# Experts in a mixture layer: row units of 128, 144 and 152 rows in place of 128 and 152

## The chip, the core and the metric

The kernel runs on one core of a Trainium2 chip. The metric is the device time of one launch in microseconds. Three runs of the kernel before gave 4332.75, 4333.61 and 4339.43 us; their median, 4333.61 us, is its time. The profiled execution took 4334.02 us, and its span, from the first to the last recorded instruction, is 4332.2 us. Engines are called as in the profile: PE (matmul) with PEld (its weight loads), DVE (vector), ACT (scalar), POOL (GpSimd) and SP (which issues most DMAs).

## What is computed

512 tokens of width 1024 in fp32 run through two blocks: retention and gated attention, a dense feed-forward, a second gated mixer, a mixture of experts, then a second block with two kinds of attention and a lookup of expert rows (called `peer` in the names). The change is in the mixture of experts:

```python
def moe_swiglu(h, w_router, w_gate, w_up, w_down):
    logits = (xt @ w_router).astype(jnp.float32)          # 512 x 8
    top_logits, top_idx = lax.top_k(logits, TOP_K)         # 2 of 8
    gates = jax.nn.softmax(top_logits, axis=-1)
    order = jnp.argsort(top_idx.reshape(-1))
    group_sizes = jnp.bincount(flat_e, length=N_EXPERTS)
    xs = xt[order // TOP_K]                                # 1024 rows, by expert
    hid = silu(ragged_dot(xs, w_gate, group_sizes)) * ragged_dot(xs, w_up, group_sizes)
    ys = lax.ragged_dot(hid, w_down, group_sizes)          # weights 1024x3584 and 3584x1024 per expert
```

The 1024 rows (512 tokens, two experts each) spread over eight experts as the router decides. On the inputs of the reference its router gives the experts 0 to 7 these numbers of rows: 137, 118, 116, 149, 142, 117, 118, 127.

## The kernel before

Routing, up to the counts, is done at run time: `Router.route` (L1667 to 1757) on DVE takes the two best of eight logits per token, counts the rows of each expert (`count`), and decides with which units an expert is computed. An expert with at most 128 rows takes one unit of 128 rows (kind A), one with more takes units of 152 (kind B). `need` holds the units per expert and kind, `upto` their running sum, `owner` the expert of each unit, `begin` the first row of an expert in the list of rows. The list `token_of_row` in DRAM has a region for each kind: A from row 0, B from row `FIRST_ROW[1]` = 1024. Once the casts to `R.units` and `R.expert` are done (L1722, L1724), every engine reads the number of units of each kind into a register (`expert_values`, lower bound 1) and loops over them. The rest of the routing makes `router_here`, a 0/1 matrix by which PE gathers the rows of the first unit (L1649), and the row numbers, by which POOL scatters the tokens to the list (L1661).

A unit goes through the 3584 hidden columns of its expert in 14 groups of 256. For each group SP loads 1 MB of gate, up and down weights (L1869, L1870, L1876) into one of two rooms, as soon as PE frees it. PE multiplies, for each half j of 128 columns, 8 gate and 8 up matmuls (L1891; the weights are stationary, the unit's rows the moving columns), ACT takes silu (L1984), DVE multiplies (L2014), and PE adds the down product. Kind A has the hidden rows as stationary and 512 weight columns moving (L1908); kind B has the weights stationary and its rows moving (L1921), so that its output is transposed. At the end of a B unit DVE copies the sums to `yT` (L2042), PE turns them back (L1974), and ACT stores them to `y_rows`; meanwhile POOL has fetched the next unit's rows by an index (L1800, L1804), PE turns them (`turn`, L1816) and DVE places them (`place`, L1827). Groups 1 to 12 of a unit run in an inner loop of six passes with two groups each, the units of a kind in an outer loop. First all A units run, then all B units.

`y_rows` (3072 rows, `ROWS_MAX`) is blanked by one DMA from SP (L582), issued in the retention stage at 220 us and waited for at the end of the gated stage behind it (`Clears.end`, L587). Kinds have their own rooms and signals (`ExpertRows`).

Of the kernel before, what the change touches and what calls it, by code (L numbers as in the profile page):

```python
# [33 lines left out]
UNIT_ROWS = (P, 152)  # L34
GROUP = 256
UNITS_MAX = (N_EXP, (2 * T + (N_EXP - 1) * (UNIT_ROWS[1] - 1)) // UNIT_ROWS[1])
FIRST_ROW = (0, UNITS_MAX[0] * UNIT_ROWS[0])
ROWS_MAX = (FIRST_ROW[1] + UNITS_MAX[1] * UNIT_ROWS[1] + P - 1) // P * P
# [1547 lines left out]
class Router:  # L1586
# [19 lines left out]
    def rooms(self, st):  # L1606
# [14 lines left out]
        self.need = S.sb("router_need", [P, 2, N_EXP], F32, st)  # L1621
        self.large = S.sb("router_large", [P, N_EXP], F32, st)
        self.begin = S.sb("router_begin", [P, 2, N_EXP], F32, st)
        self.more = S.sb("router_more", [P, N_EXP], F32, st)
        self.upto = S.sb("router_upto", [P, 2, N_EXP], F32, st)
# [4 lines left out]
        self.past = S.sb("router_past", [P, 2, 16, N_EXP], F32, st)  # L1630
        self.owner = S.sb("router_owner", [P, 2, 16], F32, st)
# [34 lines left out]
    def route(self, dve):  # L1666
        S, R, nc, ps, own = self.S, self.R, self.S.nc, self.S.ps, self.own  # L1667
        lg, top, top_i, top_f, hot, both, e2 = self.lg, self.top, self.top_i, self.top_f, self.hot, self.both, self.e2
        need, large, begin, more, upto, first, pos = self.need, self.large, self.begin, self.more, self.upto, self.first, self.pos
# [42 lines left out]
        dve.wait_ge(own.sem, o.value())  # L1712
        nc.vector.tensor_tensor(begin[:, :, :], upto[:, :, :], need[:, :, :], ALU.subtract).then_inc(own.sem, o.up())
        for c in range(2):
            nc.vector.tensor_tensor(self.past[:, c, :, :], S.const("iota16").unsqueeze(2).broadcast_to([P, 16, 8]),
                                    upto[:, c, :].unsqueeze(1).broadcast_to([P, 16, 8]), ALU.is_ge).then_inc(own.sem, o.up())
# [8 lines left out]
        for c in range(2):  # L1725
            nc.vector.tensor_scalar(begin[:, c, :], begin[:, c, :], float(UNIT_ROWS[c]), float(FIRST_ROW[c]), ALU.mult,
                                    ALU.add).then_inc(own.sem, o.up())
# [3 lines left out]
        nc.vector.tensor_tensor(begin[:, 0, :], begin[:, 0, :], need[:, 0, :], ALU.mult).then_inc(own.sem, o.up())  # L1731
        nc.vector.tensor_tensor(begin[:, 1, :], begin[:, 1, :], large[:, :], ALU.mult).then_inc(own.sem, o.up())
        dve.wait_ge(own.sem, o.value())
        nc.vector.tensor_tensor(first[:, :], begin[:, 0, :], begin[:, 1, :], ALU.add).then_inc(own.sem, o.up())
        dve.wait_ge(own.sem, o.value())
# [29 lines left out]

class ExpertRows:


    def __init__(self, S, R, size, st):
        self.S, self.R = S, R  # L1770
        self.unfetched = 1 if size == 0 else 0
        self.rows, self.row0 = UNIT_ROWS[size], FIRST_ROW[size]
        self.subs = [(r0, min(P, self.rows - r0)) for r0 in range(0, self.rows, P)]
        self.bank0 = (2, 4)[size]
        n = len(self.subs)
        self.xg = S.sb(f"rows{size}_x", [P, n, D], F32, st)
        self.xu = S.sb(f"rows{size}_xt", [P, KD, self.rows], F32, st)
# [11 lines left out]

    def units(self, eng):  # L1790
        size = 0 if self.row0 == 0 else 1
        return expert_values(eng, self.R.units[0:1, size:size + 1], 1, UNITS_MAX[size])

    def fetch(self, pool, u):
        S, nc, R, n_subs = self.S, self.S.nc, self.R, len(self.subs)

        pool.wait_ge(self.turned.sem, self.turned.at(2 * n_subs * u))
        settle(pool, S.sig("passed_pool"))
        for s, (r0, n) in enumerate(self.subs):
            pool.dma_start(self.index[0:n, s:s + 1], R.token_of_row[bass.ds(u * self.rows + self.row0 + r0, n), :]).then_inc(self.indexed.sem, 16)  # L1800
        pool.wait_ge(self.indexed.sem, self.indexed.at(16 * n_subs * (u + (1 - self.unfetched))))
        settle(pool, S.sig("passed_pool"))
        for s, (r0, n) in enumerate(self.subs):
# [4 lines left out]
    def turn(self, pe, u):  # L1808
        S, nc = self.S, self.S.nc
        pe.wait_ge(self.gathered.sem, self.gathered.at(16 * len(self.subs) * (u + (1 - self.unfetched))))  # L1810
        settle(pe, S.sig("passed_pe"))
        for s, (r0, n) in enumerate(self.subs):
# [7 lines left out]
    def place(self, dve, u):  # L1820
        S, nc, n_subs = self.S, self.S.nc, len(self.subs)
        for s, (r0, n) in enumerate(self.subs):
            for half in range(2):
                dve.wait_ge(self.turned.sem, self.turned.at(2 * n_subs * u + 2 * s + half + 1))
# [5 lines left out]
    def store(self, act, u):  # L1830
        for s, (r0, n) in enumerate(self.subs):
            act.dma_start(self.R.y[bass.ds(u * self.rows + self.row0 + r0, n), :], self.yrow[0:n, s, :]).then_inc(self.stored.sem, 16)


def experts_stage(S, R, router, xn):
# [5 lines left out]
    with ExitStack() as st:  # L1841
# [3 lines left out]
        gs = S.sb("experts_gs", [P, 2, UNIT_ROWS[1]], F32, st)  # L1845
        hid = S.sb("experts_hid", [P, 2, UNIT_ROWS[1]], F32, st)
        yT = S.sb("experts_yt", [P, KD, UNIT_ROWS[1]], F32, st)
        zero = S.sb("experts_zero", [P, BANK], BF16, st)
        A, B = ExpertRows(S, R, 0, st), ExpertRows(S, R, 1, st)
        router.rooms(st)  # L1850
        routed = router.routed

        with nc.Block("experts") as block:
            @block.sync
            def _(sp):
                def unit(E, size, u, others=None, n_others=0):
                    e = expert_values(sp, R.expert[0:1, size, bass.ds(u, 1)], 0, N_EXP - 1)
                    g, up, dn = (a[w][0][bass.ds(e, 1)].rearrange("o a b -> (o a) b")
                                 for w in ("moe_w_gate", "moe_w_up", "moe_w_down"))
                    with sp.Fori(0, per) as i:  # L1860
                        for b in range(2):
# [3 lines left out]
                            sp.wait_ge(E.freed[b].sem, E.freed[b].at(u * per + i))  # L1865
# [8 lines left out]
                            sp.wait_ge(E.down_freed[b].sem, E.down_freed[b].at(u * per + i))  # L1874
# [4 lines left out]
                n_a, n_b = A.units(sp), B.units(sp)  # L1879
                with sp.Fori(0, n_a) as u:  # L1880
                    unit(A, 0, u)
                with sp.Fori(0, n_b) as u:
                    unit(B, 1, u, A, n_a)

            @block.tensor
            def _(pe):
                def gate_up(E, b, n, j):
                    pe.wait_ge(E.hidden[j].sem, E.hidden[j].at(n))
                    for w, bank in ((wg, 4 + j), (wu, 6 + j)):
                        for k in range(KD):  # L1890
                            ins = nc.tensor.matmul(ps[bank][:, 0:E.rows], w[:, b, k, j * P:(j + 1) * P], E.xu[:, k, :],  # L1891
# [22 lines left out]
                def down_b(b, u, i, n):  # L1914
                    for j in range(2):
                        pe.wait_ge(B.hidden[j].sem, B.hidden[j].at(n + 1))
                        if j == 0:
                            pe.wait_ge(B.down_loaded[b].sem, B.down_loaded[b].at((u * per + i + 1) * 16))
                        for d in range(KD):
                            at = (d % 2) * B.rows  # L1920
                            ins = nc.tensor.matmul(ps[d // 2][:, at:at + B.rows], wd[:, b, j, d * P:(d + 1) * P], hid[:, j, :],  # L1921
                                                   start=False, stop=False, skip_group_check=True)
                            if j == 0 and d == 0:
                                ins.then_inc(B.freed[b].sem, 1)
                    ins.then_inc(B.down_freed[b].sem, 1)
# [3 lines left out]
                n_a, n_b = A.units(pe), B.units(pe)  # L1929
# [20 lines left out]
                with pe.Fori(0, n_b) as u:  # L1950
                    pe.wait_ge(B.x_ready.sem, B.x_ready.at(4 * u + 4))
                    settle(pe, S.sig("passed_pe"))
                    n0 = u * n_groups
                    first_half(B, 0, u, 0, n0)
                    pe.wait_ge(B.emitted.sem, B.emitted.at(4 * u))
                    for bank in range(4):
                        nc.tensor.matmul(ps[bank][:, :], zero[:, 0:P], zero[:, :], start=True, stop=False, skip_group_check=True)
                    down_b(0, u, 0, n0)
                    with pe.Fori(0, per - 1) as i:
                        first_half(B, 1, u, i, n0 + i * 2 + 1)  # L1960
                        down_b(1, u, i, n0 + i * 2 + 1)
                        first_half(B, 0, u, i + 1, n0 + i * 2 + 2)
                        down_b(0, u, i + 1, n0 + i * 2 + 2)
                    first_half(B, 1, u, per - 1, n0 + last)
# [1828 lines left out]
```

## Time and profile before

| | us |
|---|---|
| median of three runs | 4333.61 |
| profiled execution | 4334.02 |
| its span | 4332.2 |
| expert units, 128 rows (5) | 1307.6 to 2067.4 |
| expert units, 152 rows (3) | 2067.4 to 2603.5 |

The page of the profile gives the busy time of each engine over the span, and a strip of 40 slices of 108 us, each digit a busy share in tenths. Views by window give the same for any stretch, with the granted clock of PE (1.00 is 2.4 GHz) and the share and rate of the DMA engines. The timeline lists instructions in order of time, with start and length, merged when they repeat (xN), and in brackets how long the engine had been idle before and what released it. An fp32 matmul leaves two records. A length of one matmul includes its way through the array, so the distance from one start to the next is what it costs in a stream.

### The profile page before, as it was taken

The numbers are of one execution on the slowest core, as the hardware profiler recorded it, in microseconds if no ns is written. First come the engines' busy times: TensorE is split into PE (matmuls) and PEld (weight loads), VectorE is DVE, ScalarE is ACT, GpSimd is POOL, SyncE is SP. The second block draws the span as 40 slices with busy tenths as digits, with TensorE's granted clock in tenths as the row PEclk, the third lists the DMA queues.
The fourth block names the chain that finished last, engine by engine and source line by source line (L and its number), as shares of the span: only waits on it lengthen the run. The fifth ranks groups of instructions, "written<-read, shape, count | busy, mean of one in ns | idle before, by whom it ended". The sixth has DMA issues, their size and how long they took to land. (4 is left out here: it accounts for less than half of the span.)

```text
span 4332.2 us, 45502 instructions
## 1 busy us (share of the span) xinstructions
PE 3776.8 (87%) x17099; PEld 2506.9 (58%) x17106; DVE 1706.8 (39%) x3683; ACT 626.6 (14%) x1566; POOL 1095.9 (25%) x1162
## 2 busy tenths in 40 slices
PE   7989999999989999999999996998866777666666
PEld 3465777744747888888999993465422222222222
DVE  2051231013730000000000004748887776877655
ACT  1121000013520000000000003143211111111011
POOL 0010000001400000000000000003667777777775
PEclk9989999999989999999999998989888888888888
DMA  3143675230019888898777764036899999999998
GB/s 114 48 166 120 229 257 189 98 136 0 20 68 275 306 294 303 306 311 298 254 258 250 257 215 140 25 103 240 337 392 386 418 416 414 419 416 416 419 415 355
DMA packets 549127, 1092.57 MB, mean 252 GB/s; under 512 B 37577, under 2 KB 336982, under 8 KB 548870
## 3 DMA queue, kind: packets, MB, share of 16 engines
q1 hardware_dynamic: 395802, 539.66, 36.8%
q0 software_dynamic: 150768, 546.25, 31.3%
q10 hardware_dynamic: 2428, 5.03, 0.3%
q8 instruction: 69, 1.13, 0.1%
q14 instruction: 60, 0.49, 0.0%
HBM read 1069.55 MB, written 21.30 MB: 252 GB/s over the span
## 5 line engine op out<-in xcount | busy, mean ns | idle before, releaser
L3224 PE MATMUL banks<-peer_ring,consts 128*128 128x512 f32 x1512 | 846.9, 721 | 372.8 <-DMA peer_ring<-in_peer_v_dram,peer_expert 372.8
L3224 PEld LDWEIGHTS banks<-peer_ring,consts 128*128 128x128 f32 x1512 | 339.2, 232 | 875.1 <-DMA peer_ring<-in_peer_v_dram,peer_expert 465.2
L3425 DVE SCALAR_TENSOR_TENSOR peer_ring<-peer_ring,banks 128x1024 f32<-128x1024 f32 x512 | 594.1, 1217 | 252.4 <-DMA peer_ring<-in_peer_u_dram,peer_expert 251.5
L3128 POOL DMA_INDIRECT peer_ring<-in_peer_u_dram,peer_expert x512 | 482.4, 942 | 546.3 <-POOLq L2745 347.1
L3128 POOL DMA_INDIRECT peer_ring<-in_peer_v_dram,peer_expert x512 | 490.6, 958 | 170.1 <-issue 142.5
L2014 DVE TENSOR_TENSOR experts_hid<-experts_gs,banks 128x128 f32<-128x128 f32 (+1 forms) x224 | 66.7, 298 | 1175.9 <-ACT experts_gs L1984 1175.9
L1891 PEld LDWEIGHTS banks<-rows_xt,experts_wg 128*128 128x128 f32 x3584 | 446.9, 192 | 45.2 <-issue 45.1
L1891 PE MATMUL banks<-rows_xt,experts_wg 128*128 128x128 f32 (+1 forms) x3584 | 462.3, 282 | 11.3 <-DMA experts_wu<-in_moe_w_up_dram 9.3
L1891 PE MATMUL banks<-rows_xt,experts_wu 128*128 128x128 f32 (+1 forms) x3584 | 461.3, 282 | 0.0
L1891 PEld LDWEIGHTS banks<-rows_xt,experts_wu 128*128 128x128 f32 x3584 | 441.2, 192 | 0.0
L405 PE MATMUL banks<-xT,proj_w 128*128 128x512 f32 (+1 forms) x720 | 319.6, 601 | 8.2 <-PEq L3576 4.8
L1800 POOL DMA_DIRECT2D rows_index<-token_of_row x13 | 7.4, 575 | 1061.2 <-PE banks L1816 1043.0
L1908 PE MATMUL banks<-experts_wd,experts_hid 128*128 128x512 f32 x560 | 251.9, 592 | 0.0
L405 PEld LDWEIGHTS banks<-xT,proj_w 128*128 128x128 f32 (+1 forms) x720 | 135.5, 190 | 185.2 <-issue 183.9
L1023 POOL TENSOR_TENSOR hgrn_both<-k,hgrn_diff 128x256 f32<-128x256 f32 x56 | 44.3, 814 | 772.7 <-ACT hgrn_diff L934 761.6
L1984 ACT ACTIVATE experts_gs<-banks 128x128 f32<-128x128 f32 (+1 forms) x224 | 63.9, 285 | 1183.1 <-PE banks L1891 1183.0
L3456 DVE SCALAR_TENSOR_TENSOR banks<-peer_ring,peer_wgt,banks 128x1024 f32<-128x1024 f32 x130 | 167.5, 1288 | 79.3 <-DMA peer_ring<-in_peer_v_dram,peer_expert 78.7
L1921 PE MATMUL banks<-experts_hid,experts_wd 128*128 128x152 f32 x1344 | 180.5, 293 | 0.0
L1921 PEld LDWEIGHTS banks<-experts_hid,experts_wd 128*128 128x128 f32 x1344 | 176.3, 190 | 0.4
L408 PE MATMUL banks<-proj_w,xT 128*128 128x512 f32 (+1 forms) x448 | 174.1, 548 | 0.0
L1357 PE MATMUL banks<-xT,ffn_wg 128*128 128x256 f32 x704 | 161.3, 383 | 1.2 <-ACT ada_c L1395 1.2
L1431 DVE TENSOR_TENSOR ffn_hid<-ffn_gs,banks 128x256 f32<-128x256 f32 x44 | 18.5, 422 | 360.9 <-ACT ffn_gs L1401 360.9
(506 smaller groups left out, 3754.7 us busy)
## 6 DMA issues: line engine op xcount, KB each, us to landing
experts_wg<-in_moe_w_gate_dram SPq DMA_DIRECT2D x112, 1024.0 KB, 5.2
experts_wu<-in_moe_w_up_dram SPq DMA_DIRECT2D x112, 1024.0 KB, 7.7
experts_wd<-in_moe_w_down_dram SPq DMA_DIRECT2D x112, 1024.0 KB, 8.1
ada_w<-in_w_ada_dram SPq DMA_DIRECT2D x12, 2048.0 KB, 7.9
ffn_wg<-in_ffn_w_gate_dram SPq DMA_DIRECT2D x22, 1024.0 KB, 7.8
ffn_wu<-in_ffn_w_up_dram SPq DMA_DIRECT2D x22, 1024.0 KB, 10.4
ffn_wd<-in_ffn_w_down_dram SPq DMA_DIRECT2D x22, 1024.0 KB, 11.8
y_rows<-blank SPq DMA_DIRECT2D x1, 12288.0 KB, 41.8
```

Of the source, the lines that this page charges most:

```text
L405: last = nc.tensor.matmul(out_of(g), wk[:, m * P:m * P + width], xT[:, k, :], start=(k == 0), stop=(k == KD - 1))
L408: last = nc.tensor.matmul(out_of(g), xT[:, k, m * P:(m + 1) * P], wk[:, 0:n], start=(k == 0), stop=(k == KD - 1))
L1357: last = nc.tensor.matmul(ps[bank][:, 0:ROWS], w[:, b, k, j * P:(j + 1) * P], xT[:, k, u * ROWS:(u + 1) * ROWS], start=(k == 0), stop=(k = ...
L1891: ins = nc.tensor.matmul(ps[bank][:, 0:E.rows], w[:, b, k, j * P:(j + 1) * P], E.xu[:, k, :], start=(k == 0), stop=(k == KD - 1))
L1908: ins = nc.tensor.matmul(ps[hf][:, :], hid[:, j, 0:P], wd[:, b, j, hf * 512:(hf + 1) * 512], start=(first and j == 0), stop=(final and j = ...
L1921: ins = nc.tensor.matmul(ps[d // 2][:, at:at + B.rows], wd[:, b, j, d * P:(d + 1) * P], hid[:, j, :], start=False, stop=False, skip_group_ ...
L1984: nc.scalar.activation(gs[:, j, 0:E.rows], ps[4 + j][:, 0:E.rows], ACT.Silu).then_inc(E.gated[j].sem, 1)
L2014: nc.vector.tensor_tensor(hid[:, j, 0:E.rows], gs[:, j, 0:E.rows], ps[6 + j][:, 0:E.rows], ALU.mult).then_inc(E.hidden[j].sem, 1)
L3128: pool.indirect_dma_start(out=ring[:, slot_of(kind, n, b), :], out_offset=None, in_=tables[kind == "value"], in_offset=bass.IndirectOffset ...
L3224: last = nc.tensor.matmul(ps[bank + hf][:, :], diag[:, n % 2 * B + b, :], ring[:, slot_of("value", n, b), hf * 512:(hf + 1) * 512], start= ...
L3425: nc.vector.scalar_tensor_tensor(row, row, 1.0, rows_at, ALU.mult, ALU.mult, accum_out=acts[:, t % 2, at:at + 1]).then_inc(dotted[q].sem, 1)
L3456: ins = nc.vector.scalar_tensor_tensor(sum_at, row, weight(n, b), sum_at, ALU.mult, ALU.add)
```

## The change

There are three kinds of unit: A with 128 rows, B with 144, C with 152. An expert with 129 to 144 rows takes one B unit, one with 145 to 152 one C unit, one with more several C units. B and C lie behind each other in the list of rows: B from `FIRST_LARGE` = 1024, C from 1024 + 144 x (number of B units), with the numbers of B units and C units each at least 1. C shares the rooms, the signals and the weight buffers of B: it has an `ExpertRows` of its own with the same tiles, and its units are numbered on from those of B (`number`). The body of a wide unit becomes a function (`large_units`) that PE, ACT and DVE run twice, for B and for C. Rows are fetched, turned and placed by 152 for both kinds (`fetched`); the matmuls, silu, product, the copy to `yT`, the turn back and the store go by the kind's own rows. `y_rows` grows from 3072 to 4096 rows and the token list from 3328 to 4352. The routing computes three `need`, `upto`, `past` and `begin` in place of two, each engine reads three counts.

The diff, cut to its core:

```diff
-UNIT_ROWS = (P, 152)
+UNIT_ROWS = (P, 144, 152)
+SIZES = len(UNIT_ROWS)
...
-FIRST_ROW = (0, UNITS_MAX[0] * UNIT_ROWS[0])
-ROWS_MAX = (FIRST_ROW[1] + UNITS_MAX[1] * UNIT_ROWS[1] + P - 1) // P * P
+FIRST_LARGE = UNITS_MAX[0] * UNIT_ROWS[0]
+ROWS_MAX = (FIRST_LARGE + UNITS_MAX[1] * UNIT_ROWS[1] + UNITS_MAX[2] * UNIT_ROWS[2] + P - 1) // P * P
...
-        nc.vector.tensor_scalar(need[:, 0, :], count, 0.0, None, ALU.is_gt).then_inc(own.sem, o.up())
-        nc.vector.tensor_scalar(large[:, :], count, float(UNIT_ROWS[0]), None, ALU.is_gt).then_inc(own.sem, o.up())
-        nc.vector.tensor_scalar(need[:, 1, :], count, float(UNIT_ROWS[0]), None, ALU.is_gt).then_inc(own.sem, o.up())
+        for c, low in enumerate((0, UNIT_ROWS[0], UNIT_ROWS[1])):
+            nc.vector.tensor_scalar(above[:, c, :], count, float(low), None, ALU.is_gt).then_inc(own.sem, o.up())
+        for m in (1, 2, 3):
+            nc.vector.tensor_scalar(more[:, m - 1, :], count, float(m * UNIT_ROWS[2]), None, ALU.is_gt).then_inc(own.sem, o.up())
         dve.wait_ge(own.sem, o.value())
-        nc.vector.tensor_tensor(need[:, 0, :], need[:, 0, :], large[:, :], ALU.subtract).then_inc(own.sem, o.up())
-        for m in range(1, (T + UNIT_ROWS[1] - 1) // UNIT_ROWS[1]):
-            nc.vector.tensor_scalar(more[:, :], count, float(m * UNIT_ROWS[1]), None, ALU.is_gt).then_inc(own.sem, o.up())
+        nc.vector.tensor_tensor(need[:, 0:2, :], above[:, 0:2, :], above[:, 1:3, :], ALU.subtract).then_inc(own.sem, o.up())
+        nc.vector.tensor_tensor(need[:, 2, :], above[:, 2, :], more[:, 0, :], ALU.add).then_inc(own.sem, o.up())
+        for m in (1, 2):
             dve.wait_ge(own.sem, o.value())
-            nc.vector.tensor_tensor(need[:, 1, :], need[:, 1, :], more[:, :], ALU.add).then_inc(own.sem, o.up())
-            dve.wait_ge(own.sem, o.value())
-        for c in range(2):
+            nc.vector.tensor_tensor(need[:, 2, :], need[:, 2, :], more[:, m, :], ALU.add).then_inc(own.sem, o.up())
+        dve.wait_ge(own.sem, o.value())
+        for c in range(SIZES):
             nc.vector.tensor_tensor_scan(upto[:, c, :], S.const("ones")[:, 0:8], need[:, c, :], 0.0, ALU.mult,
...
+        nc.vector.scalar_tensor_tensor(begin[:, 2, :], upto[:, 1, N_EXP - 1:N_EXP].broadcast_to([P, N_EXP]), float(UNIT_ROWS[1]),
+                                       begin[:, 2, :], ALU.mult, ALU.add).then_inc(own.sem, o.up())
...
         nc.vector.tensor_tensor(first[:, :], begin[:, 0, :], begin[:, 1, :], ALU.add).then_inc(own.sem, o.up())
+        dve.wait_ge(own.sem, o.value())
+        nc.vector.tensor_tensor(first[:, :], first[:, :], begin[:, 2, :], ALU.add).then_inc(own.sem, o.up())
...
+    def number(self, u, narrower):
+        return u + narrower if self.size == 2 else u
+
+    def row(self, u, narrower):
+        row = u * self.rows + self.row0
+        return row + narrower * UNIT_ROWS[1] if self.size == 2 else row
...
         A, B = ExpertRows(S, R, 0, st), ExpertRows(S, R, 1, st)
+        C = ExpertRows(S, R, 2, st, narrower=B)
...
-                    unit(B, 1, u, A, n_a)
+                    unit(B, u, u, A, n_a)
+                with sp.Fori(0, n_c) as u:
+                    unit(C, u, C.number(u, n_b))
...
-                            ins = nc.tensor.matmul(ps[bank][:, 0:E.rows], w[:, b, k, j * P:(j + 1) * P], E.xu[:, k, :],
+                            ins = nc.tensor.matmul(ps[bank][:, 0:E.rows], w[:, b, k, j * P:(j + 1) * P], E.xu[:, k, 0:E.rows],
...
+                def large_units(E, n_units, narrower=0):
+                    with pe.Fori(0, n_units) as u:
+                        w = E.number(u, narrower)
+                        pe.wait_ge(E.x_ready.sem, E.x_ready.at(4 * w + 4))
...
+                large_units(B, n_b)
+                large_units(C, n_c, n_b)
```

## Rows read from the trace of the kernel before

**Rows 1.** The page: busy time of each engine over the span.

```profile
PE 3776.8 (87%) x17099; PEld 2506.9 (58%) x17106; DVE 1706.8 (39%) x3683; ACT 626.6 (14%) x1566; POOL 1095.9 (25%) x1162
```

**Rows 2.** Windows: start:end, length, busy PE, PEld, DVE, ACT, POOL; clock, DMA share, GB/s.

```profile
1455.00:1610.00 155.00, 155.00 (x1062) 127.40 (x1061) 10.85 (x33) 9.34 (x30) 1.56 (x2) 1.00 0.89 303
...
2067.00:2246.00 179.00, 178.12 (x1380) 177.18 (x1381) 12.30 (x38) 8.35 (x28) 3.47 (x5) 1.00 0.76 257
```

**Rows 3.** Waits of PE from 1455 to 2603 us: total, times, longest.

```profile
PE banks L1891 <- DVE rows_xt L1827: 2.0, 1, 2.0
PE banks L1974 <- DVE experts_yt L2042: 1.1, 3, 0.4
```

**Rows 4.** Groups by line and form, PE: count, busy us, mean ns.

```profile
L1891 PE MATMUL banks<-rows_xt,experts_wg 128*128 128x128 f32 x2240 | 274.7, 276 | 9.3 <-DMA experts_wu<-in_moe_w_up_dram 9.3
...
L1891 PE MATMUL banks<-rows_xt,experts_wg 128*128 128x152 f32 x1344 | 187.6, 293 | 2.0 <-DVE rows_xt L1827 2.0
...
L408 PE MATMUL banks<-proj_w,xT 128*128 128x144 f32 x64 | 8.3, 286 | 0.0
```

**Rows 5.** Timeline of PE: one group of a 152-row unit, and the next two starts.

```profile
2080.80 2.23 PE L1891 MATMUL banks<-rows_xt,experts_wg 128*128 128x152 f32 x16
...
2089.07 4.30 PE L1921 MATMUL banks<-experts_hid,experts_wd 128*128 128x152 f32 x32
...
2093.20 2.23 PE L1891 MATMUL banks<-rows_xt,experts_wg 128*128 128x152 f32 x16
...
2105.60 2.23 PE L1891 MATMUL banks<-rows_xt,experts_wg 128*128 128x152 f32 x16
```

**Rows 6.** Timeline: 144-column matmuls of a projection, and what follows.

```profile
2669.07 2.12 PE L408 MATMUL banks<-proj_w,xT 128*128 128x144 f32 x16
2671.03 1.02 PE L542 MATMUL banks<-iq,consts 128*128 128x512 f32 x2
```

**Rows 7.** Timeline: DVE for half 1 of that group.

```profile
2089.67 0.31 DVE L2014 TENSOR_TENSOR experts_hid<-experts_gs,banks 128x152 f32<-128x152 f32 x1 [3.82 <-ACT experts_gs L1984]
```

**Rows 8.** Timeline: from one 152-row unit to the next, and the start of the third.

```profile
2242.38 0.37 SPq L1876 DMA_DIRECT2D experts_wd<-in_moe_w_down_dram  x1
2242.51 1.62 DVE L2042 COPY experts_yt<-banks 128x304 f32<-128x304 f32 x4 [3.80 <-PE banks L1966]
...
2246.11 2.33 PE L1891 MATMUL banks<-rows_xt,experts_wg 128*128 128x152 f32 x16
...
2256.01 0.38 SPq L1869 DMA_DIRECT2D experts_wg<-in_moe_w_gate_dram  x1
...
2424.73 2.33 PE L1891 MATMUL banks<-rows_xt,experts_wg 128*128 128x152 f32 x16
```

**Rows 9.** Timeline: routing, the first weight load and the second group.

```profile
1289.53 0.17 DVE L1699 TENSOR_SCALAR router_need<-router_tiles 128x8 f32<-128x8 f32 x1
...
1291.18 0.25 DVE L1710 TENSOR_TENSOR_SCAN router_upto<-consts,router_need 128x8 f32<-128x8 f32 x2
...
1292.08 0.42 DVE L1718 TENSOR_REDUCE router_owner<-router_past 128x32 f32<-128x256 f32 x1
...
1292.83 0.18 DVE L1724 CAST expert_of<-router_owner 128x32 int32<-128x32 f32 x1
...
1295.65 0.41 SPq L1869 DMA_DIRECT2D experts_wg<-in_moe_w_gate_dram  x1
...
1326.64 3.77 PE L1891 MATMUL banks<-rows_xt,experts_wg 128*128 128x128 f32 x16 [8.19 <-DMA experts_wu<-in_moe_w_up_dram]
```

**Rows 10.** DMA issues of the page; a window; SP's timeline behind the blanking.

```profile
y_rows<-blank SPq DMA_DIRECT2D x1, 12288.0 KB, 41.8
...
262.00:290.00 28.00, 28.00 (x175) 19.04 (x172) 13.89 (x26) 6.52 (x12) 7.16 (x8) 0.97 0.00 1
...
314.93 1.01 SPq L1132 DMA_DIRECT2D ada_w<-in_ab_w_out_dram  x2
```

**Rows 11.** Timeline: the first matmuls of the retention stage.

```profile
218.91 4.55 PE L618 MATMUL banks<-qa,ka 128*128 128x512 f32 x16 [0.94 <-PEq L383]
```

More of the change, by code:

```diff
@@ L1620, in rooms @@
         self.upto_tile = S.sb("router_tiles", [P, TT, N_EXP], F32, st)
[L1621 to L1625, printed above, removed]
+        self.need = S.sb("router_need", [P, SIZES, N_EXP], F32, st)
+        self.above = S.sb("router_above", [P, SIZES, N_EXP], F32, st)
+        self.begin = S.sb("router_begin", [P, SIZES, N_EXP], F32, st)
+        self.more = S.sb("router_more", [P, 3, N_EXP], F32, st)
+        self.upto = S.sb("router_upto", [P, SIZES, N_EXP], F32, st)
         self.first = S.sb("router_first", [P, N_EXP], F32, st)
@@ L1668, in route @@
         lg, top, top_i, top_f, hot, both, e2 = self.lg, self.top, self.top_i, self.top_f, self.hot, self.both, self.e2
-        need, large, begin, more, upto, first, pos = self.need, self.large, self.begin, self.more, self.upto, self.first, self.pos
+        need, above, begin, more, upto, first, pos = self.need, self.above, self.begin, self.more, self.upto, self.first, self.pos
         o = Count(own)
@@ L1763, in close, with parts_of, __init__ @@
             s.base += n
+def parts_of(rows):
+    return [(r0, min(P, rows - r0)) for r0 in range(0, rows, P)]
 class ExpertRows:
-    def __init__(self, S, R, size, st):
-        self.S, self.R = S, R
+    def __init__(self, S, R, size, st, narrower=None):
+        self.S, self.R, self.size = S, R, size
         self.unfetched = 1 if size == 0 else 0
-        self.rows, self.row0 = UNIT_ROWS[size], FIRST_ROW[size]
-        self.subs = [(r0, min(P, self.rows - r0)) for r0 in range(0, self.rows, P)]
-        self.bank0 = (2, 4)[size]
+        self.rows, self.row0 = UNIT_ROWS[size], FIRST_LARGE if size else 0
+        self.subs = parts_of(self.rows)
+        self.fetched = self.subs if size == 0 else parts_of(UNIT_ROWS[2])
+        self.bank0 = 4 if size else 2
+        if narrower is not None:
+            self.share(narrower)
+            return
         n = len(self.subs)
         self.xg = S.sb(f"rows{size}_x", [P, n, D], F32, st)
-        self.xu = S.sb(f"rows{size}_xt", [P, KD, self.rows], F32, st)
+        self.xu = S.sb(f"rows{size}_xt", [P, KD, UNIT_ROWS[2] if size else P], F32, st)
         self.yrow = S.sb(f"rows{size}_y", [P, n, D], F32, st)
@@ L1788, in __init__, with share @@
             self.y_ready, self.y_turned, self.emitted = sig("y_ready"), sig("y_turned"), sig("emitted")
-    def units(self, eng):
[L1791 to L1797, printed above, removed]
+    def share(self, B):
+        self.xg, self.xu, self.yrow, self.index = B.xg, B.xu, B.yrow, B.index
+        self.indexed, self.gathered, self.turned, self.stored, self.x_ready = B.indexed, B.gathered, B.turned, B.stored, B.x_ready
+        self.loaded, self.freed, self.down_loaded, self.down_freed = B.loaded, B.freed, B.down_loaded, B.down_freed
+        self.hidden, self.gate_up, self.gated = B.hidden, B.gate_up, B.gated
+        self.y_taken, self.y_ready, self.y_turned, self.emitted = B.y_taken, B.y_ready, B.y_turned, B.emitted
@@ new lines, in units, with fetch @@
+    def units(self, eng):
+        return expert_values(eng, self.R.units[0:1, self.size:self.size + 1], 1, UNITS_MAX[self.size])
+    def number(self, u, narrower):
[3 more added lines that the diff above has]
+        return row + narrower * UNIT_ROWS[1] if self.size == 2 else row
+    def fetch(self, pool, u, narrower=0):
+        S, nc, R, n_subs, w, row = self.S, self.S.nc, self.R, len(self.fetched), self.number(u, narrower), self.row(u, narrower)
+        pool.wait_ge(self.turned.sem, self.turned.at(2 * n_subs * w))
@@ L1798, in fetch @@
         settle(pool, S.sig("passed_pool"))
-        for s, (r0, n) in enumerate(self.subs):
-            pool.dma_start(self.index[0:n, s:s + 1], R.token_of_row[bass.ds(u * self.rows + self.row0 + r0, n), :]).then_inc(self.indexed.sem, 16)
-        pool.wait_ge(self.indexed.sem, self.indexed.at(16 * n_subs * (u + (1 - self.unfetched))))
+        for s, (r0, n) in enumerate(self.fetched):
+            pool.dma_start(self.index[0:n, s:s + 1], R.token_of_row[bass.ds(row + r0, n), :]).then_inc(self.indexed.sem, 16)
@@ L1818, in turn, with place @@
                 last.then_inc(self.turned.sem, 1)
-    def place(self, dve, u):
-        S, nc, n_subs = self.S, self.S.nc, len(self.subs)
-        for s, (r0, n) in enumerate(self.subs):
+    def place(self, dve, w):
+        S, nc, n_subs = self.S, self.S.nc, len(self.fetched)
+        for s, (r0, n) in enumerate(self.fetched):
             for half in range(2):
-                dve.wait_ge(self.turned.sem, self.turned.at(2 * n_subs * u + 2 * s + half + 1))
+                dve.wait_ge(self.turned.sem, self.turned.at(2 * n_subs * w + 2 * s + half + 1))
                 src = S.ps[self.bank0 + 2 * s + half][:, :].rearrange("p (k r) -> p k r", k=4)[:, :, 0:n]
@@ L1987, in _, with large_units @@
                 act.wait_ge(routed.sem, routed.at(2))
-                n_a, n_b = A.units(act), B.units(act)
+                def large_units(E, n_units, narrower=0):
+                    with act.Fori(0, n_units) as u:
+                        w = E.number(u, narrower)
+                        for g in range(n_groups):
+                            silu(E, w, g, 0)
+                            silu(E, w, g, 1)
+                        act.wait_ge(E.emitted.sem, E.emitted.at(4 * w + 4))
+                        settle(act, S.sig("passed_act"))
+                        E.store(act, u, narrower)
+                n_a, n_b, n_c = A.units(act), B.units(act), C.units(act)
                 with act.Fori(0, n_a) as u:
@@ L2019, in _ @@
                 dve.wait_ge(routed.sem, routed.at(2))
-                n_a, n_b = A.units(dve), B.units(dve)
+                n_a, n_b, n_c = A.units(dve), B.units(dve), C.units(dve)
                 A.place(dve, 0)
@@ L2033, in _ @@
                 B.place(dve, 0)
[L2034 to L2052 removed]
+                large_units(B, n_b)
+                large_units(C, n_c, n_b)
             @block.gpsimd
@@ L2063, in _ @@
                     B.fetch(pool, u + 1)
+                with pool.Fori(0, n_c) as u:
+                    C.fetch(pool, u + 1, n_b)
 class Routing:
```

184 lines of the change are left out of this document (91 added, 93 removed).

## The prediction, made before any run of the change

> **What bounds the kernel now.** I read the page first: PE is busy 87% of the span, twice any other engine [rows 1]. The change touches only the expert stage (1307 to 2603 us), the routing just ahead of it, and one blanking transfer at 220 us, so I went on by windows. A window in the 128-row units (1455 to 1610 us) and the window of a 152-row unit (2067 to 2246) show PE busy for all but 0.9 us, a granted clock of 1.00 (the 2.4 GHz level), and a DMA share of 0.89 in the narrow units against 0.76 in the wide one [rows 2]. So a wide unit is set by PE alone: ACT and DVE are busy 8 and 12 us of 179 beside it. The waits agree: from 1455 to 2603 us PE waited 2.0 us once, on entering the wide loop, and 1.1 us in three pieces for `yT` [rows 3].
>
> How many units there are: the groups by form have 2240 gate matmul records with 128 columns and 1344 with 152 [rows 4]. A unit issues 14 groups x 2 halves x 8 k = 224 gate matmuls and each leaves two records (fp32), 448. So 5 narrow units and 3 wide ones, eight for eight experts: each expert has one unit, three of them with 129 to 152 rows. Which of the three have at most 144, the trace can't say (padding is computed as well). That comes from the reference: its router on its own inputs gives 137, 118, 116, 149, 142, 117, 118 and 127 rows. Five are at most 128, three above, as the trace has it. By the new sizes: five units of 128, two of 144 (137 and 142), one of 152 (149). No kind is empty, so the lower bound of one unit per kind adds none.
>
> **The matmuls of two units: the gain.** A 152-row unit has 3 x 448 = 1344 records (gate, up and down alike have the rows as moving columns). One group of 96 takes 12.40 us (2080.80 to 2093.20), 129.2 ns a record [rows 5]. For 144 columns this kernel has its own row, of another stage but with the same kind of operands (fp32 rows moving against 128x128 weights): 16 records from 2669.07 to 2671.03, 122.5 ns each [rows 6]. The difference is 6.7 ns, which is 16 cycles of 2.4 GHz: two for each column left out. The mean lengths of single records say the same in coarser numbers, 293 ns for 152 columns, 286 for 144, and 276 for 128; a straight line from 128 to 152 gives 5.7 ns for 8 columns [rows 4]. I take the row with the very width: 2 x 1344 x 6.7 ns = 17.9 us, and 15.2 us as the low end, from the line.
>
> What would be late next in such a unit? Not the weights: three 1 MB loads in 96 x 122.5 ns = 11.8 us are 267 GB/s, and the narrow units draw 303 without PE waiting [rows 2, 3]. Not the activation chain: ACT and DVE end the hidden rows of half 1 at 2089.98, 0.91 us after the down matmuls of half 0 began (2089.07) [rows 5, 7], and those will take 16 x 122.5 ns = 1.96 us. The clock: narrow units, with still shorter matmuls, ran at 1.00 [rows 2].
>
> **The unit's tail.** Between units PE waits 0.4 us [rows 3] for the four copies of 304 columns into `yT`, 1.62 us together [rows 8]; at 288 columns they take 16/304 less, 0.09 us, on the path, in two units: 0.2 us at most, I take 0.1. Rows are still gathered, turned and placed by 152, and the transposes back still have 128 columns: nothing.
>
> **A third loop.** The 152-row code now stands in a loop of its own behind the 144-row one. On PE any extra time at the entry is exposed: between two wide units it waits only for `yT`. Entering the wide loop from the narrow one showed 2.0 us, ended by DVE's placing of rows; a cost under that would be hidden there [rows 3]. So 0 to 2.0 us; I take 0.2, since the edge most like it, from unit to unit in the same loop, shows none. The row numbers `u + n_b` are register adds beside matmuls of 122 ns. The others have cover: at a unit's start SP's next weight load is issued 13.6 us after the one before (2242.38, 2256.01) [rows 8], and ACT, DVE and POOL wait there for PE. An entry that costs SP less is hidden; beyond it the weights come late by the difference.
>
> **Routing.** It is on the path: the first weight load is issued 2.64 us after the last cast ends (1293.01, 1295.65), and PE's second group (1326.64) waits 8.19 us for weights [rows 9]. DVE up to the cast: the steps of `need` took 1.65 us (1289.53 to 1291.18) for ten operations; seven starts in it (the scan behind them is the last) wait for the operation before. A waiting step costs about 0.20 us and another 0.08. New: six comparisons, then need, need, add, add: 5 x 0.08 + 4 x 0.20 + 0.09 = 1.29, less by 0.36. From the first scan to the reduction two scans, `begin` and two `past` took 0.90 (1291.18 to 1292.08); a third scan and `past` add 0.35. The reduction has 384 elements for 256 (0.42): 0.13, wider casts 0.02. Together +0.14. Then SP reads three unit counts in place of two; two counts, one expert number and the address took 2.64 us, so one is at most 0.88; I take 0.4. The rest of the routing grows by some 0.5 us (a third scaling, the shift of `begin`, a second addition) and delays `router_here`, hence PE's gather of the first unit: its first group may start 0.5 us later, but the second's wait of 8.19 us covers it. Scatter and first fetch on POOL lie behind that too. Sum +0.5 us, between 0.1 and 1.0.
>
> **Blanking.** `y_rows` grows from 3072 to 4096 rows. The transfer took 41.8 us for 12288 KB, so 55.7 for 16384: it lands near 276 us in place of 262. From 262 to 290 us the DMA share is 0.00, and SP, which waits for it, issues nothing until 314.93, held by PE [rows 10]. Nothing; 39 us of cover, and if it were gone, 14 us.
>
> **Sum.** -17.9 - 0.1 + 0.2 + 0.5 = -17.3 us. The profiled execution was 4334.02 us, span 4332.2; it becomes 4316.7. The median of the runs is 0.4 below it: 4316.3. The stages behind start as a whole that much earlier.
>
> **Rivals.**
> 1. Narrower matmuls don't run closer together, because weight loads set the rate: PEld is busy 177 of 179 us [rows 2]. Then only +0.6 is left: 4334.2. Against it stands the 122.5 ns row, with the same loads [rows 6]. Chance 0.02. The Trainium skill, TensorE: Matmul & The Clock Gate, section Back-to-back issue gap, has a rule this way: in streams of load and matmul the gap is set by both, 81 ns at 128 columns and 131 at 512, so 0.13 ns a column. By it an estimate of the gain is 2688 x 8 x 0.13 ns = 2.8 us. The rows of this kernel have 0.7 to 0.8 ns a column [rows 4 to 6].
> 2. An expert stands in another class on the chip (142 is two rows from the limit): one 144 unit, half the gain, 4325.2. Chance 0.015.
> 3. Slower, an empty kind: if all three large experts had at most 144 rows, or all more, the missing kind would still run one unit, since the count is at least 1. 149 would have to fall by 5, or 137 rise by 8. Price a whole unit, 170 to 179 us, less what the narrower ones give: 4334 + 152 = 4486 or more. Chance 0.015.
> 4. Slower, code fetching: the third body moves the loops, and each backward jump could cost PE a fetch. There are about 7 such jumps in each of 8 units, 56; a start of new code elsewhere showed PE held 0.94 us by its queue [rows 11]. 56 x 0.94 = 53 us, so 4316 + 53 = 4369; from 0.33 us a jump the gain is gone. Against it: groups start 12.40 us apart whether a jump lies between them (2093.20 to 2105.60) or not [rows 5]. Chance 0.02. The Trainium skill, Runtime: NRT & Kernel Launch, section Instruction fetch mechanics, says that a taken branch to code outside the window of two fetched pages stalls; the present loops don't show it.
> 5. The blanking is exposed after all: 4330. Chance 0.01.
>
> **How the numbers follow.** The forecast has 0.91: 4316.3, of itself 4313.5 to 4321.5: at the low end 17.9 and 0.2 saved, entry 0, routing 0.1, and 2 us between medians; at the high end 15.2 saved, entry 2.0 and routing 1.0. That leaves out under 2 in 10, so it is the range. Within 0.2% (8.7 us, about what a measurement can tell from no change) lie rivals 1, 2 and 5, with a little for unknown costs: 0.05. Slower: rivals 3 and 4, 0.04. Faster: 0.91.
>
> **What would show it.** In the profile after: 896 gate records of 144 columns and 448 of 152; groups of 11.76 us in the first two wide units; unit starts 169.6 us apart for the first two, against 178.6 now (2246.11 to 2424.73) [rows 8]; no idle of PE ahead of the last unit's first matmul beyond that before each other one; the first weight load 6.7 us after the first comparison of the counts, against 6.1 now (1289.53 to 1295.65) [rows 9]; blank landing near 276 us with no wait at 315. Wrong it would be with a rate above 124 ns, a ninth unit, or a PE wait for weights in the 144 units.

## The result: 12 us slower, with the predicted gain inside it

The changed kernel takes 4346.0 us (median of 8 runs, 4341.18 to 4348.73), the kernel before 4334.3 in the runs beside it: a ratio of 1.0023, interval 1.0013 to 1.0032. Forecast were 4316.3 us, 17.3 less than before. The profiled execution of the changed kernel took 4347.47 us, its span is 4345.8.

The tile view of the lookup's ring, and those of the gathered expert rows and of the stores, give the ends of three stretches. Columns: line, engine, operation, count, min/median/max ns, first and last start. Before:

```profile
L2117 POOL DMA_INDIRECT qb<-y_rows,row_of x2: 937/954/971, 2609.8 to 2611.1; - x2
L3128 POOL DMA_INDIRECT peer_ring<-in_peer_u_dram,peer_expert x512: 932/937/1512, 2967.2 to 4273.8; - x171
L3106 SPq DMA_DIRECT2D out_dram<-h x4: 332/335/356, 3556.0 to 4329.2; - x4
```

After:

```profile
L2166 POOL DMA_INDIRECT qb<-y_rows,row_of x2: 941/958/974, 2595.1 to 2596.4; - x2
L3177 POOL DMA_INDIRECT peer_ring<-in_peer_u_dram,peer_expert x512: 935/941/1551, 2951.1 to 4286.4; - x171
L3155 SPq DMA_DIRECT2D out_dram<-h x4: 332/335/356, 3551.1 to 4342.7; - x4
```

| stretch | before, us | after, us | difference |
|---|---|---|---|
| up to the first expert weight load | 1295.7 | 1299.5 | +3.8 |
| from there to the first gather of expert rows | 1314.1 | 1295.6 | -18.5 |
| to the first gather into `peer_ring` | 357.4 | 356.0 | -1.4 |
| lookup stage, to the last store | 1362.0 | 1391.6 | +29.6 |

So the stretch of the expert units gave about what was forecast (of which pieces is told below), and a stage that the change doesn't name took back 30 us. The windows from 3100 to 4250 us, inside the lookup stage, show how (start:end, length, busy PE, PEld, DVE, ACT, POOL, clock, DMA share, GB/s); before, then after:

```profile
3100.00:4250.00 1150.00, 793.06 (x1496) 321.85 (x1498) 850.50 (x1767) 147.09 (x450) 852.94 (x898) 0.84 1.01 412
```

```profile
3100.00:4250.00 1150.00, 788.46 (x1464) 318.06 (x1466) 833.69 (x1732) 141.45 (x434) 831.58 (x878) 0.83 1.01 402
```

The DMA engines are full in both, at 412 GB/s and at 402, and the other engines ran about 2% fewer instructions in the same time (ACT 4%). From 2965 us to the end PE waited 372.8 us for rows of the ring before and 388.8 after. The packets of that window tell the same; before, then after:

```profile
DMA packets 129935, 473.41 MB, mean 412 GB/s; under 512 B 14433, under 2 KB 14433, under 8 KB 129896
```

```profile
DMA packets 127038, 462.85 MB, mean 402 GB/s; under 512 B 14113, under 2 KB 14113, under 8 KB 126999
```

The mix is the same and the packets are longer: 16 engines x 1150 us x 1.01 / 129935 is 143 ns for one before, 146 after. The stage gathers rows of 4096 bytes into the rooms of `peer_ring`, and nothing of that is in the diff. What is in it, and was left out of the core shown above and of the prediction, is this line:

```diff
-    R.expert = S.sb("expert_of", [P, 2, 16], I32, st)
+    R.expert = S.sb("expert_of", [P, SIZES, 16], I32, st)
     R.units = S.sb("n_units", [P, 80], I32, st)[:, 0:SIZES]
```

`expert_of` lives for the whole kernel and is 64 bytes per partition larger. Tiles are laid one behind the other, so all that come later start 64 bytes further. By the addresses in the built programs, `peer_ring` started at byte 133376 of each partition, a multiple of 256 (521 x 256), and now at 133440, 64 past one. `n_units`, which uses 2 (now 3) of its 80 numbers, is where a distance can be made up. The weight rooms `experts_wg`, `experts_wu` and `experts_wd` start 224 bytes past a multiple of 256 in the kernel before and 32 past one in the changed kernel.

### The profile page after: what moved, and what is told of

Read it like the earlier page. It is cut to its first block and busy times, and to the rows that moved or that the text cites. A ratio compares the mean times of both kernels' runs of the same rounds, so it can differ in the third digit from the quotient of the medians.

```text
span 4345.8 us, 45478 instructions
## 1 busy us (share of the span) xinstructions
PE 3775.3 (87%) x17099; PEld 2495.2 (57%) x17106; DVE 1706.5 (39%) x3688; ACT 626.4 (14%) x1566; POOL 1094.6 (25%) x1162
## 5 line engine op out<-in xcount | busy, mean ns | idle before, releaser
L3273 PE MATMUL banks<-peer_ring,consts 128*128 128x512 f32 x1512 | 858.9, 730 | 388.8 <-DMA peer_ring<-in_peer_v_dram,peer_expert 388.8
L2056 DVE TENSOR_TENSOR experts_hid<-experts_gs,banks 128x128 f32<-128x128 f32 (+2 forms) x224 | 66.2, 296 | 1158.3 <-ACT experts_gs L2021 1158.3
L1923 PE MATMUL banks<-rows_xt,experts_wg 128*128 128x128 f32 (+2 forms) x3584 | 457.4, 281 | 10.2 <-DMA experts_wu<-in_moe_w_up_dram 8.2
L1923 PE MATMUL banks<-rows_xt,experts_wu 128*128 128x128 f32 (+2 forms) x3584 | 454.9, 280 | 0.0
L2021 ACT ACTIVATE experts_gs<-banks 128x128 f32<-128x128 f32 (+2 forms) x224 | 63.5, 284 | 1164.6 <-PE banks L1923 1164.5
L1953 PE MATMUL banks<-experts_hid,experts_wd 128*128 128x144 f32 (+1 forms) x1344 | 174.5, 288 | 0.0
L1432 DVE TENSOR_TENSOR ffn_hid<-ffn_gs,banks 128x256 f32<-128x256 f32 x44 | 18.5, 421 | 360.4 <-ACT ffn_gs L1402 360.4
## 6 DMA issues: line engine op xcount, KB each, us to landing
y_rows<-blank SPq DMA_DIRECT2D x1, 16384.0 KB, 53.9
```

What stands on the lines that cost most here:

```text
L1953: ins = nc.tensor.matmul(ps[d // 2][:, at:at + E.rows], wd[:, b, j, d * P:(d + 1) * P], hid[:, j, 0:E.rows], start=False, stop=False, skip ...
L2021: nc.scalar.activation(gs[:, j, 0:E.rows], ps[4 + j][:, 0:E.rows], ACT.Silu).then_inc(E.gated[j].sem, 1)
L2056: nc.vector.tensor_tensor(hid[:, j, 0:E.rows], gs[:, j, 0:E.rows], ps[6 + j][:, 0:E.rows], ALU.mult).then_inc(E.hidden[j].sem, 1)
L3273: last = nc.tensor.matmul(ps[bank + hf][:, :], diag[:, n % 2 * B + b, :], ring[:, slot_of("value", n, b), hf * 512:(hf + 1) * 512], start= ...
```

## Experiments

There are three theories: the place of the tiles in SBUF (1), the larger tables in DRAM (2), and the code (3). The first four kernels tell them apart. In what follows "before" is the kernel before, run beside each.

**The old places restored.** By the addresses of the built program all tiles are back where they were, except `n_units` itself, the router's own tiles, and eight tiles of the first block (`ret_probs` and those called `gla_`), which stand 32 bytes further. All tiles of the lookup stage are among those restored.

```diff
-    R.units = S.sb("n_units", [P, 80], I32, st)[:, 0:SIZES]
+    R.units = S.sb("n_units", [P, 64], I32, st)[:, 0:SIZES]
```

> The changed kernel with `n_units` 64 wide in place of 80, so that every tile behind it in SBUF stands where it stood before the change; `expert_of` had grown by 64 bytes per partition. In the profiled pair the lookup stage (first peer_u gather to the last store of the output) took 1362.0 us before and 1391.6 after, and everything up to its start was 16.1 us shorter. Theory 1 (the tiles' places): the lookup stage is back at about 1362 us and the gain stays, 4316 to 4319 us. Theory 2 (DRAM: y_rows and the list are larger, all that lies behind them is moved) and theory 3 (the code: a third loop and more instructions ahead of the stage): the stage stays at about 1391 us and the time at 4341 to 4349.

The kernel took 4317.6 us (4316.52 to 4320.8), ratio 0.9955 (0.9942 to 0.9969). The lookup stage took 1363.2 us:

```profile
L3177 POOL DMA_INDIRECT peer_ring<-in_peer_u_dram,peer_expert x512: 934/941/1813, 2949.6 to 4257.2; - x171
L3155 SPq DMA_DIRECT2D out_dram<-h x4: 333/336/357, 3540.4 to 4312.8; - x4
```

Code and DRAM tables are those of the changed kernel, so theories 2 and 3 fall, and rival 4 of the prediction (jumps that fetch code) with them. This version is faster than both kernels.

**The same shift in the kernel before.**

```diff
-    R.units = S.sb("n_units", [P, 80], I32, st)[:, 0:2]
+    R.units = S.sb("n_units", [P, 96], I32, st)[:, 0:2]
```

> The kernel before with `n_units` 96 wide in place of 80: nothing but every later tile in SBUF moved by 64 bytes, as in the changed kernel. Theory 1: the lookup stage takes about 1391 us, the whole 4334 + 30 = 4364 us, with up to 3 us more if the late start of the expert stage (1295.65 to 1299.47 us) is of the same cause. Theories 2 and 3: 4334 us, no difference.

It took 4363.4 us, ratio 1.0065 (1.0052 to 1.0079), and the lookup stage 1393.6 us. The first expert load was at 1295.6 us, where it is without the shift. So this profile gives no sign that the 3.8 us late start of the changed kernel comes from the shift; that one execution can't exclude it, since the start varies by some us, as is seen below.

**Larger tables in the kernel before.**

```diff
-ROWS_MAX = (FIRST_ROW[1] + UNITS_MAX[1] * UNIT_ROWS[1] + P - 1) // P * P
+ROWS_MAX = 4096
```

> The kernel before with y_rows of 4096 rows and a list of 4352, both blanked, as in the changed kernel, and two kinds of unit. Theory 2: lookup stage about 1391 us, whole 4364 us. Theories 1 and 3: 4334 us. Blanking itself: the transfer lands 12 us later with 39 us of cover, so 0; if the gated mixer beside it is slowed by it, up to 2 us (the load behind that stage was issued 1.63 us later in the changed kernel).

It took 4335.4 us, ratio 0.9998 (0.9989 to 1.0007), and the lookup stage 1362.7 us. Neither place nor blanking of the tables in DRAM costs anything that can be measured; the load behind the gated stage was issued at 314.0 us (314.9 before).

**Only the ring moved.**

```diff
+        S.sb("ring_pad", [P, 16], F32, st)
         ring = S.sb("peer_ring", [P, 2 * B, D], F32, st)
```

> The kernel before with an unused tile of 64 bytes per partition right ahead of `peer_ring`: the ring and the few tiles behind it move by 64 bytes, everything of the stages before stays. Theory 1 in its narrow form (the start of the ring's rooms decides, since the stage is bound by the row loads into them): lookup stage about 1391 us, whole 4364 us. If another moved tile is at fault: 4334 us here and 4364 in the kernel in which all tiles moved. Theories 2 and 3: 4334 us.

It took 4363.6 us, ratio 1.0059 (1.0045 to 1.0072), and the lookup stage 1392.3 us. The whole cost lies with the ring and the eight tiles behind it, which moved too. Of those eight a DMA writes only `later_q_in`, once, before this window begins (at 2979.9 us in the kernel before, landing 25.7 us later). The window:

```profile
3100.00:4250.00 1150.00, 789.64 (x1470) 319.17 (x1472) 833.66 (x1740) 143.20 (x436) 833.78 (x879) 0.83 1.01 402
```

All stages ahead are untouched here, and yet the copy to `router_lg` came at 1289.6 us, against 1285.5 before. Over all kernels here it lies between 1283.4 and 1289.6, and kernels that differ only in tiles of the lookup stage span that whole range. In the changed kernel it came at 1288.7, so 3.2 us of its 3.8 us late start lie inside this spread; the rest is the routing.

**How far off, and which grid.** The same unused tile with 8, 32, 48 and 64 numbers moves the ring by 32, 128, 192 and 256 bytes.

> The kernel before with 128 unused bytes per partition ahead of `peer_ring`; 64 bytes cost 28 to 30 us. Theory P (a packet whose start lies off the grid is one piece longer, whatever the distance; grid of 256 bytes): again 28 to 30 us, 4363 us. Theory Q (the cost grows with the distance from the grid, as the share of 32-byte steps that the first piece reads in vain would have it): twice as much, 4390 us. Theory R (the grid is 128 bytes): no cost, 4335 us. The Trainium skill, DMA: Bandwidth & Descriptors, section How a descriptor splits into AXI transactions, has a grid of 256 bytes and counts steps of 32 bytes; by it an estimate of a 4096-byte row is 128 steps on the grid, 130 at 64 bytes past it and 132 at 128, so 1.6 and 3.1% of the stage.

> The kernel before with 256 unused bytes per partition ahead of `peer_ring`: the ring then starts on a multiple of 512 bytes, while in the kernel before it starts 256 past one. With a grid of 256 bytes: no cost, 4335 us. If the sheer presence of another tile or the distance itself were at fault: 4363 us or more. If the grid is 512 and the kernel before already pays: faster, by up to 28 us.

> The kernel before with 32 unused bytes per partition ahead of `peer_ring`. Theory P (one piece more, whatever the distance): 4363 us. Theory Q (cost by distance): half of that of 64 bytes, 4349 us.

> The kernel before with 192 unused bytes per partition ahead of `peer_ring`. Theory P: 4363 us. Theory Q: three times the cost of 64 bytes, 4419 us.

| bytes past a multiple of 256 | lookup stage, us | GB/s, 3100 to 4250 | median, us | ratio and interval |
|---|---|---|---|---|
| 0 (before) | 1362.0 | 412 | 4336.4 | |
| 32 | 1391.2 | 402 | 4367.2 | 1.0072 (1.0055 to 1.0089) |
| 64 | 1392.3 | 402 | 4363.6 | 1.0059 (1.0045 to 1.0072) |
| 128 | 1392.2 | 403 | 4362.4 | 1.0059 (1.0042 to 1.0076) |
| 192 | 1390.8 | 402 | 4365.6 | 1.0063 (1.0047 to 1.0080) |
| 0 (256 further) | 1365.4 | 410 | 4335.4 | 0.9998 (0.9989 to 1.0008) |

The 64-byte row is the run above, beside which the kernel before took 4335.5 us. Theory P (one price at any distance) holds, Q (a price that grows with the distance) and R (a grid of 128 bytes) fall: a ring is on the grid or off it, with the same price of about 29 us for 32 bytes as for 192. Moving by 256 costs nothing that the medians show, so neither the extra tile nor a grid of 512 is at work (the ring before starts at 256 past a multiple of 512, the moved one on one). Its profiled execution was the slowest of its ten (4346.72 us), so its 1365.4 us and 410 GB/s may be that execution's and not the place's. What in the chip makes a packet longer stays open; only the rule was measured.

**The size of the gain, once more.**

```diff
-UNIT_ROWS = (P, 144, 152)
+UNIT_ROWS = (P, 142, 150)
```

> The changed kernel with the tiles at their old places, and unit sizes 128, 142 and 150 in place of 128, 144 and 152 (the largest experts have 137, 142 and 149 rows). By the term of the prediction (two cycles of 2.4 GHz for each column left out, 0.83 ns): 3 x 1344 x 2 x 0.83 = 6.7 us less than the 4317.6 of the kernel with 144 and 152, so 4311 us. If only the step from 152 to 144 gave something and weight loads set the rate below: no difference.

It took 4308.0 us (4303.74 to 4314.28), ratio 0.9941 (0.9927 to 0.9955). That is below the 4311 expected, but the runs spread over 10 us. The rate is sharper. PE's timeline, two starts of a group with 142 columns and two with 150:

```profile
2087.84 2.10 PE L1923 MATMUL banks<-rows_xt,experts_wg 128*128 128x142 f32 x16
...
2099.43 2.10 PE L1923 MATMUL banks<-rows_xt,experts_wg 128*128 128x142 f32 x16
```

```profile
2436.09 2.21 PE L1923 MATMUL banks<-rows_xt,experts_wg 128*128 128x150 f32 x16
...
2448.36 2.21 PE L1923 MATMUL banks<-rows_xt,experts_wg 128*128 128x150 f32 x16
```

11.59 and 12.27 us for 96 records are 120.7 and 127.8 ns; with 122.5 for 144 and 129.2 for 152 [rows 5, 6], 0.7 to 0.9 ns a column all along. Sizes so close to the counts of one input are of no use beyond it.

**Do the weight rooms pay too?** With the tiles at their old places they start 224 bytes past the grid.

```diff
+        S.sb("weights_pad", [P, 8], F32, st)
         wg = S.sb("experts_wg", [P, 2, KD, GROUP], F32, st)
```

> The changed kernel with the tiles at their old places and 32 unused bytes per partition ahead of `experts_wg`, so that the three weight rooms start on multiples of 256 bytes (they start 224 past one, in the kernel before too); their packets are pieces of 1 KB for gate and up and of 4 KB for down. If the same grid holds for loads from SP: less DMA share in the narrow units than 0.88 at the same GB/s, by at least the 2 to 3% that the ring's rows show and more for 1 KB pieces, and a shorter wait of PE for the second group's weights (6.8 to 8.2 us). The whole: 0 to 3 us less than 4317.6, since PE sets the expert units. If the grid holds for POOL's queue alone: no difference in either.

The window of narrow units from 1460 to 1610 us, without and with the 32 bytes (both with the tiles at their old places):

```profile
1460.00:1610.00 150.00, 150.00 (x1027) 123.22 (x1026) 10.84 (x33) 9.33 (x30) 1.56 (x2) 1.00 0.89 303
```

```profile
1460.00:1610.00 150.00, 150.00 (x1027) 123.22 (x1027) 10.54 (x32) 9.05 (x29) 1.56 (x2) 1.00 0.84 303
```

The same 303 GB/s came with a share of 0.84 in place of 0.89, which is 6% less DMA time, and a 1 MB load of `experts_wu` landed after 7.1 us in place of 7.6, one of `experts_wd` after 7.4 in place of 8.1. So the place of the room counts for loads from SP too. The changed kernel, whose rooms start 32 past the grid, has the same share of 0.89 at 303 GB/s, so here too the distance makes no difference:

```profile
1460.00:1610.00 150.00, 150.00 (x1028) 123.22 (x1027) 10.56 (x32) 9.06 (x29) 1.56 (x2) 1.00 0.89 303
```

That the grid is 256 bytes, and not a part of it, was measured for the ring alone, since neither 224 nor 32 is a multiple of 64. The kernel with the pad took 4313.5 us, ratio 0.9949 (0.9936 to 0.9963), beside 0.9955 (0.9942 to 0.9969) without it. The intervals overlap, since PE sets these units. Whether the shorter wait for the second group (6.3 us, beside 9.2) is the pad's doing can't be said: other kernels with the rooms at 224 show 5.6 to 9.6.

## The prediction, step by step

**Matmul term: right.** One group in the changed kernel:

```profile
2083.45 2.12 PE L1923 MATMUL banks<-rows_xt,experts_wg 128*128 128x144 f32 x16
...
2091.29 4.08 PE L1953 MATMUL banks<-experts_hid,experts_wd 128*128 128x144 f32 x32
2095.21 2.12 PE L1923 MATMUL banks<-rows_xt,experts_wg 128*128 128x144 f32 x16
```

A group took 11.76 us, as forecast, for 12.40 [rows 5]; over 28 groups that is 17.9 us. The 144-column row of another stage [rows 6] gave the rate exactly; the line through the mean lengths [rows 4] would have been 15% short. Rival 1 (weight loads set the rate) is refuted. The Trainium skill's rule of 0.13 ns a column, cited there, doesn't hold for these fp32 pairs: 0.7 to 0.9 ns were measured.

**Unit counts: right.** The groups by form have 896 gate records with 144 columns and 448 with 152, so each of the three experts stands in the class that the reference's counts gave, and no kind is empty; rivals 2 and 3 did not occur.

```profile
L1923 PE MATMUL banks<-rows_xt,experts_wg 128*128 128x144 f32 x896 | 120.2, 288 | 2.0 <-DVE rows_xt L1855 2.0
```

**The tail and the third loop: right, the entry is free.** PE's timeline at the start of the second 144-row unit, and at the start of the last unit:

```profile
2238.55 1.94 PE L1985 MATMUL banks<-consts,experts_yt 128*128 128x128 f32 x16 [0.32 <-DVE experts_yt L2069]
2240.32 2.22 PE L1923 MATMUL banks<-rows_xt,experts_wg 128*128 128x144 f32 x16
```

```profile
2408.14 1.94 PE L1985 MATMUL banks<-consts,experts_yt 128*128 128x128 f32 x16 [0.32 <-DVE experts_yt L2069]
...
2409.92 2.33 PE L1923 MATMUL banks<-rows_xt,experts_wg 128*128 128x152 f32 x16
```

It took 169.6 us from unit to unit (178.6 before [rows 8]), the wait for `yT` 0.32 in place of 0.38, and from the start of the transposes to the first matmul of the new loop it took 1.78 us, against 1.77 between the two units of one loop (2238.55 to 2240.32). I had put 0.2 us on the entry; it is 0. The whole list of PE's waits from 1455 us on is that of before [rows 3] to 0.1 us:

```profile
PE banks L1923 <- DVE rows_xt L1855: 2.0, 1, 2.0
PE banks L1985 <- DVE experts_yt L2069: 1.0, 3, 0.4
```

**The first wide unit: 1.7 us that the sum doesn't have.** From its first matmul (2069.06) to that of the second unit (2240.32) it took 171.3 us and not the 169.6 forecast. PE had waited 2.0 us for its rows, and then the granted clock was 0.66 for 3 us and 0.77 for the next 3, a mixture of its two levels (1.00 is 2.4 GHz, 0.50 is 1.2 GHz), before it was 1.00 again. In the kernel before the same wait was followed by a clock of 1.00. First the timeline at that place, before and after:

```profile
2067.44 2.33 PE L1891 MATMUL banks<-rows_xt,experts_wg 128*128 128x152 f32 x16 [1.98 <-DVE rows_xt L1827]
```

```profile
2069.06 3.35 PE L1923 MATMUL banks<-rows_xt,experts_wg 128*128 128x144 f32 x16 [2.01 <-DVE rows_xt L1855]
```

Then the first 3 us of the unit, before and after:

```profile
2067.40:2070.40 3.00, 2.96 (x23) 2.97 (x24) 0.00 (x0) 0.00 (x0) 0.00 (x0) 1.00 1.09 369
```

```profile
2069.00:2072.00 3.00, 2.94 (x16) 2.95 (x17) 0.00 (x0) 0.00 (x0) 0.00 (x0) 0.66 1.08 361
```

The change isn't the cause: the kernel before with 4096 rows shows 0.63 at this place, and the one with sizes 142 and 150 shows 1.00. So the wide units gave 16.4 us in this execution and not 18.0, and 2.2 us came from ahead of them, between the first weight load and the wide loop, where the work of a unit is what it was; half of that is a shorter wait for weights (8.2 us in place of 9.3). That the stretch came out within 1 us of the forecast is therefore in part luck, while the rate of a group is not.

**Routing: right.** From the first comparison of the counts to the first weight load it took 6.71 us (6.7 forecast, 6.12 before [rows 9]):

```profile
1292.76 0.32 DVE L1701 TENSOR_SCALAR router_above<-router_tiles 128x8 f32<-128x8 f32 x3
...
1296.09 0.19 DVE L1726 CAST expert_of<-router_owner 128x48 int32<-128x48 f32 x1
...
1299.47 0.41 SPq L1899 DMA_DIRECT2D experts_wg<-in_moe_w_gate_dram  x1
```

The split was off: DVE took 0.04 us more up to the end of the cast (3.52 in place of 3.48) and not 0.14; from the end of the cast to the first load it was 3.19 and not 2.64, so the third count costs 0.55, where I took 0.4.

**Blanking: right.** It lands 53.9 us after its issue, at 274 us (55.7 and 276 forecast), and SP's next load comes at 316.6. Rival 5 did not occur.

```profile
y_rows<-blank SPq DMA_DIRECT2D x1, 16384.0 KB, 53.9
```

**The step that failed** is the last sentence of the sum, "The stages behind start as a whole that much earlier". It took the later stages as fixed because the diff does not touch their code. But they are fixed only if their tiles keep their places, and a persistent tile had grown by 64 bytes. The missing term is +29 us, in the stage whose bound is the DMA; that stage was never costed. With the places restored the same change gave 17.9 us less than the kernel before beside it (4335.5 to 4317.6), where 17.3 were forecast; the interval is 13 to 25 us, so an agreement to 0.6 us is more than was measured. None of the five rivals had this mechanism: all of them lay in the stages that the change touches. The chance of 0.04 for slower was therefore far too small. The diff and the sizes of the tiles would have shown that the ring moves; what such a move costs, no trace at hand could tell.

Two numbers of the prediction come out a little differently when worked out again, without weight for the result: the gain is gone from 0.31 us a jump (17.3/56) and not 0.33, and its own bounds give 4313.6 and 4321.4 us for the ends of the range.

## What to carry to other kernels

Read the allocations in a diff as well as the work: a long-lived tile that grows moves every tile behind it, and a stage bound by the DMA can pay for that far from the edit. Before costing later stages at nothing, work out the start of each tile that bulk transfers write, modulo 256 bytes, before and after; an oddly sized tile like `n_units` may be there to set such a distance. And where a gain fails to show, compare the stages by their ends first: here one table of four stretches separated a sound forecast of one stage from a loss in another.

## What was not expected of the hardware

Gathered rows of 4096 bytes that start off a multiple of 256 bytes in SBUF made a stage with full DMA engines 2.2% longer (1362.0 to about 1391.6 us, 412 to 402 GB/s), equally for 32, 64, 128 and 192 bytes. The weight loads, in pieces of 1 KB and 4 KB, took 6% more DMA time for the same bytes at 224 bytes off the grid than on it (share 0.89 and 0.84 at 303 GB/s).

The Trainium skill, DMA: Bandwidth & Descriptors, section How a descriptor splits into AXI transactions, names such a grid of 256 bytes, and there the runs agree. Its count of 32-byte steps would have the cost grow with the distance, from an estimate of 0.8% at 32 bytes to 4.7% at 192; the runs show one price for all four. Its count of transactions goes, by the same kind of estimate, from 16 to 17 for a row of 4096 bytes at each of the four distances: that is as flat as the price measured, but one in sixteen is 6.3% and not 2.2%. It speaks of bytes that are fetched in vain, and here it is the end that is written that lies off the grid, so the runs don't show what its counts are worth where rows are read.
